# Expert retrieval in two layers: gathered rows against whole tables streamed through TensorE

## What is computed

```python
q = (xb @ w_q).reshape(n, 8, 2, 128)                       # 8 heads, two halves
s = einsum('thpk,pnk->thpn', q, sub_keys)                  # 128 scores for each half
s_top, i_top = top_k(s, 16)
cand_s = s_top[:, :, 0, :, None] + s_top[:, :, 1, None, :]
cand_i = i_top[:, :, 0, :, None] * 128 + i_top[:, :, 1, None, :]
best_s, best_pos = top_k(cand_s.reshape(n, 8, -1), 16)     # 16 of 256 pairs
idx = take_along_axis(cand_i.reshape(n, 8, -1), best_pos)
gate = softmax(best_s)
act = gelu(einsum('thkd,td->thk', down[idx], xb))
out = einsum('thk,thkd->td', gate * act, up[idx])
```

## Time and profile before

| what | us |
|---|---|
| three runs | 2356.95, 2358.21, 2359.39 |
| profiled execution, span | 2356.5 |
| of this, PE busy | 2048.2 |
| DVE busy | 1155.2 |
| ACT busy | 647.4 |
| POOL busy | 601.8 |

### The profile page before, as it was taken

The page is one execution under the profiler, slowest core; times in us unless marked ns, Lnnn a source line. Parts: engine busy times, 40 slices in busy tenths (PEclk is TensorE's granted clock), DMA queues, the critical chain, the costliest instruction groups (busy, mean ns, idle before and its releaser), DMA issues.

```text
span 2356.5 us, 21481 instructions
## 1 busy us (share of the span) xinstructions
PE 2048.2 (87%) x7609; PEld 981.8 (42%) x7609; DVE 1155.2 (49%) x2857; ACT 647.4 (27%) x1813; POOL 601.8 (26%) x516
## 2 busy tenths in 40 slices
PE   7999998777777888998777777779999999999998
PEld 3455664232323336664223223334445544444443
DVE  2335766676667556766676667544534311111111
ACT  2242333332333222333332333332432210000001
POOL 0001344444444431344444444430000000000000
PEclk9999999999999998999999999999999999999999
DMA  9696999999999987999999999996313399999996
GB/s 391 252 423 246 407 417 420 420 416 422 406 420 413 409 347 293 406 420 421 421 420 417 412 421 412 407 396 262 119 57 135 160 402 427 428 426 428 427 427 262
DMA packets 98201, 860.93 MB, mean 365 GB/s; under 512 B 11406, under 2 KB 11534, under 8 KB 12844
## 3 DMA queue, kind: packets, MB, share of 16 engines
q0 software_dynamic: 73728, 536.90, 55.3%
q1 hardware_dynamic: 24364, 322.62, 32.9%
HBM read 858.44 MB, written 1.05 MB: 365 GB/s over the span
## 4 chain that ended last, share of the span: by engine, by line
PE 55%; DMA 29%; DVE 7%; ACT 4%; issue 3%; POOL 2%; POOLq 0%; SPq 0%; DVEq 0%; ACTq 0%
DMA arena<-in_experts,arena 16%; PE bank L2348 16%; PE bank L2012 15%; DMA ring<-in_experts,arena 9%; PE bank L2699 9%; PE bank L2745 4%; PE bank L2709 2%; PE bank L2116 2%; DVE arena L1479 2%; DMA arena<-in_w_up 2%; ACT arena L903 2%; POOL arena L696 1%; PE bank L2128 1%; POOL ring L696 1%; DVE ring L1479 1%
## 5 line engine op out<-in xcount | busy, mean ns | idle before, releaser
L2348 PE MATMUL bank<-arena 128*128 128x512 f32 x1040 | 486.3, 612 | 128.6 <-ACT arena L903 128.6
L2348 PE MATMUL bank<-ring,arena 128*128 128x512 f32 x1008 | 472.1, 612 | 116.5 <-ACT arena L903 116.4
L696 POOL DMA_INDIRECT arena<-in_experts,arena x260 | 299.8, 1153 | 638.2 <-PE bank L2348 331.7
L1479 DVE SCALAR_TENSOR_TENSOR arena<-arena,h 128x1024 f32<-128x1024 f32 x260 | 318.7, 1226 | 231.1 <-DMA arena<-in_experts,arena 230.1
L1479 DVE SCALAR_TENSOR_TENSOR ring<-ring,h 128x1024 f32<-128x1024 f32 x252 | 308.9, 1226 | 217.0 <-DMA ring<-in_experts,arena 216.4
L696 POOL DMA_INDIRECT ring<-in_experts,arena x252 | 301.8, 1198 | 329.5 <-PE bank L2348 288.4
L2348 PEld LDWEIGHTS bank<-arena 128*128 128x128 f32 x1040 | 191.2, 193 | 401.6 <-ACT arena L903 201.4
L2348 PEld LDWEIGHTS bank<-ring,arena 128*128 128x128 f32 x1008 | 185.5, 193 | 384.2 <-ACT arena L903 193.9
L894 ACT ACTIVATE arena<-arena 128x2 f32<-128x2 f32 x256 | 52.1, 203 | 838.5 <-DVE arena L1479 456.1
L2699 PE MATMUL bank<-ring,arena 128*64 128x512 f32 x768 | 223.4, 592 | 2.0 <-ACT arena L1096 1.2
L903 ACT ACTIVATE arena<-const,arena 128x128 f32<-128x128 f32 x512 | 177.6, 394 | 8.4
(11 more groups left out here) (430 smaller groups left out, 1811.8 us busy)
## 6 DMA issues: line engine op xcount, KB each, us to landing
ring<-in_w_gate SPq DMA_DIRECT2D x32, 2048.0 KB, 14.8
ring<-in_mod_w SPq DMA_DIRECT2D x20, 2048.0 KB, 11.8
arena<-in_w_up SPq DMA_DIRECT2D x16, 2048.0 KB, 20.9
arena<-in_w_down SPq DMA_DIRECT2D x16, 2048.0 KB, 15.8
ring<-in_w_up SPq DMA_DIRECT2D x16, 2048.0 KB, 16.4
ring<-in_w_down SPq DMA_DIRECT2D x16, 2048.0 KB, 11.5
ring<-in_w_in SPq DMA_DIRECT2D x9, 2048.0 KB, 7.3
ring<-in_peer_w_q SPq DMA_DIRECT2D x8, 2048.0 KB, 12.3
```

The lines of the kernel that those rows point to most:

```text
L696: pool.indirect_dma_start(out=gslot(l, n), out_offset=None, in_=a["experts"], in_offset=bass.IndirectOffsetOnAxis(ap=idx_all[:, t, at:at + ...
L1479: ins = v.scalar_tensor_tensor(out=row, in0=row, scalar=1.0, in1=h[:, t], op0=ALU.mult, op1=ALU.mult, accum_out=act[:, t, HEAD * hh + k:HE ...
L2348: ins = pe.matmul(bank[2 * t + c][:, :], diag[:, PER * (j % 2) + k], row[:, 512 * c:512 * c + 512], start=j % (GROUPS // NT) == 0 and k == ...
```

## The change

Both tables of a layer are read whole, once, in pieces of 1 MB, and nothing is gathered.

- The 16384 experts are 128 columns j of 128 experts i. A piece of `down` holds two columns. PE multiplies it by `hT` (8 matmuls of 256 tokens each), and ACT puts gelu of it into `kept`, 256 numbers a partition for each j, experts on the partitions. 112 columns fit (`KEPT`); the last 16 wrap onto the first once these are summed.
- A piece of `up` holds two columns as well; PE multiplies the kept products with it into the four output banks (`sums`, 4 matmuls of 512 columns for each j).
- In between, the kept products are multiplied by the gates. The picks (i, j, gate) are transposed, so that a column is a token and its 128 picks are the partitions. For 8 tokens at a time DVE makes the one-hots of i (128 wide) and of j (64 wide, half of the keys), POOL multiplies the one-hot of j by the gate, PE multiplies the two (8 matmuls, one a token, 64 columns each), which gives each token's gates by expert in a bank, and DVE multiplies 64 kept columns by it. There are 2 halves x 32 such groups a layer, with two buffers of each kind.
- Pieces go through three places (`streams`), and the last five of a layer through five more. SP's list has the pieces in the order of use, and between them the late rows of `mod_w` (all four in layer 0 now), the constants, `pool_w` and the first three chunks of `w_in`.
- Top-k works on two heads of one tile at a time, always, eight blocks a layer in a row, with 14 steps.
- The out projection is complete, and both tiles are normalised and transposed, before the first query. At a layer's end the last 8 pieces of `up` are summed for tile 0 first, then for tile 1. `keep_warm` is gone.

```diff
+TILE = 256
+KEPT = 112
+PAIR_TILES = KEYS // 2
+KEPT_PAIRS = KEPT // 2
+WRAPPED = PAIR_TILES - KEPT_PAIRS
+TAIL = 8
+STREAMS = 3
+PIECE = 2048
...
+QUERY_AT = {0: 0, 4: 1, 10: 2, 17: 3}
+ROW_AT_PAIR = {6: 16, 9: 17, 12: 18, 15: 19}
+def piece_order():
+    order = []
+    for p in range(KEPT_PAIRS):
+        if p in QUERY_AT:
+            order += [("q", 2 * QUERY_AT[p]), ("q", 2 * QUERY_AT[p] + 1)]
+        order.append(("d", p))
+    for p in range(WRAPPED):
+        order += [("u", p), ("d", KEPT_PAIRS + p)]
+    order += [("u", p) for p in range(WRAPPED, PAIR_TILES)]
+    return order
...
+    return (n + 1) % STREAMS if n < PIECES - HELD else n - (PIECES - HELD) + STREAMS
...
+EXP_AT = {29: 0, 32: 1}
+TURN_PICKS_AT = {31: 0, 34: 1}
+SPREAD = KEPT_PAIRS - 33
+GROUPS_AT = {33 + p: tuple(range(GROUPS * p // SPREAD, GROUPS * (p + 1) // SPREAD)) for p in range(SPREAD)}
+GROUPS_BEHIND = {p: tuple(range(4 * (p - WRAPPED) // 3, 4 * (p - WRAPPED + 1) // 3)) for p in range(WRAPPED, PAIR_TILES // 2)}
+TOTAL_AT = [{33 + n: n for n in range(10)}, {33: 10, 34: 11}]
...
+            def load_piece(l, n):
+                kind, i = ORDER[n]
+                k = place_of(n)
+                if k < STREAMS:
+                    same = [m for m in range(PIECES) if place_of(m) == k]
+                    at = same.index(n)
+                    if at or l:
+                        sp.wait_ge(S["piece_done"], PIECES * (l if at else l - 1) + same[at - 1] + 1)
+                    elif k == 0:
+                        sp.wait_ge(S["mixed"], NT)
+                else:
+                    sp.wait_ge(S["piece_done"], done(l, "u", KEPT_PAIRS // 2 + 7 + 4 * (k - STREAMS)))
+                sp.dma_start(streams[k], piece_source(l, kind, i)).then_inc(p_landed[k], 16)
...
+            for n in range(PIECES):
+                load_piece(0, n)
+                kind, i = ORDER[n]
+                if kind == "d" and i in (2, 5, 8, 11):
+                    load_lone(i // 3)
+                if (kind, i) == ("u", 36):
+                    sp.wait_ge(S["w_made"], 2 * GROUPS)
+                    sp.dma_start(own, a["const"][:, band_at:band_at + 2048]).then_inc(S["in_const"], 16)
+                if (kind, i) == ("u", 40):
+                    load_weights("pool", 1)
+            for n in range(PIECES):
+                load_piece(1, n)
+                if ORDER[n] == ("u", 36):
+                    load_weight(wat["in2"])
+                if ORDER[n] == ("u", 41):
+                    load_weight(wat["in2"] + 1)
+                if ORDER[n] == ("u", 46):
+                    load_weight(wat["in2_third"])
...
+                for half in range(2):
+                    for g in range(GROUPS):
+                        n = group_no(l, half, g)
+                        pool.wait_ge(S["hot_j_made"], n + 1)
+                        hot = hot_j[:, n % 2]
+                        weight = picksT[:, 2, GROUP * g:GROUP * g + GROUP].unsqueeze(2).to_broadcast([P, GROUP, HALF_KEYS])
+                        pool.tensor_tensor(hot, hot, weight, ALU.mult).then_inc(S["hot_made"], 1)
...
+                def one_hots(half, g):
+                    n = group_no(l, half, g)
+                    at = slice(GROUP * g, GROUP * g + GROUP)
+                    keys = cst("iota")[:, HALF_KEYS * half:HALF_KEYS * half + HALF_KEYS]
+                    if half == 0 and g in (0, GROUPS // NT):
+                        v.wait_ge(S["picks_ev"], NT * l + g // (GROUPS // NT) + 1)
+                    if n >= 2:
+                        v.wait_ge(S["g_done"], n - 1)
+                    i_hot, j_hot = hot_i[:, n % 2], hot_j[:, n % 2]
+                    v.tensor_tensor(i_hot, bc(cst("iota"), 1, GROUP), bc(picksT[:, 0, at], 2, KEYS), ALU.is_equal)
+                    v.tensor_tensor(j_hot, bc(keys, 1, GROUP), bc(picksT[:, 1, at], 2, HALF_KEYS), ALU.is_equal).then_inc(S["hot_j_made"], 1)
+                def weigh(half, g):
+                    n = group_no(l, half, g)
+                    if g == 0:
+                        v.wait_ge(S["s_ev"], PAIR_TILES * l + PAIR_TILES // 2 * (half + 1))
+                    v.wait_ge(S["g_done"], n + 1)
+                    runs = [(0, 0, HALF_KEYS)] if half == 0 else [(0, HALF_KEYS, KEPT - HALF_KEYS), (KEPT - HALF_KEYS, 0, KEYS - KEPT)]
+                    gates_of_keys = bank[6 + n % 2][:, :].rearrange("p (u j) -> p j u", u=GROUP)
+                    for at, v0, width in runs:
+                        part = kept_run(v0, width)[:, :, GROUP * g:GROUP * g + GROUP]
+                        ins = v.tensor_tensor(part, part, gates_of_keys[:, at:at + width], ALU.mult)
+                    ins.then_inc(S["w_made"], 1)
+                for n in range(HEADS):
+                    for step in range(STEPS):
+                        top_k(n, step)
+                    if l == 0 and n == 4:
+                        v.wait_ge(S["modp"], 4 + 20)
+                        v.tensor_tensor(mrows2, mrows1, bank[3][:, :], ALU.add).then_inc(S["rows_made"], 1)
+                gates(0)
+                for half in range(2):
+                    for g in range(GROUPS):
+                        one_hots(half, g)
+                        if (half, g) == (0, 1):
+                            gates(1)
+                        if g:
+                            weigh(half, g - 1)
+                    weigh(half, GROUPS - 1)
...
+                def add_experts(t):
+                    if t == 0:
+                        v.wait_ge(S["first_summed"], l + 1)
+                    else:
+                        v.wait_ge(S["piece_done"], PIECES * (l + 1))
+                    for c in range(2):
+                        link(v.tensor_tensor(h[:, t, 512 * c:512 * c + 512], bank[2 * t + c][:, :],
+                                             mod[:, 5, 512 * c:512 * c + 512], ALU.mult))
+                    v.tensor_tensor(x[:, t], x[:, t], h[:, t], ALU.add).then_inc(S["x_peer"], 1)
+                for t in range(NT):
+                    add_experts(t)
+                    tile_mean(("n1_1", "nf1")[l], t)
+                    if l == 0:
+                        tile_norm("n1_1", t, x, h, mod[:, 1], mod[:, 0])
+                    else:
+                        tile_gained("nf1", t, x, gvec[:, 1])
+                        tile_mean("nmix", t)
+                        tile_gained("nmix", t, h, gvec[:, 0])
...
-                    pool.indirect_dma_start(
-                        out=gslot(l, n), out_offset=None, in_=a["experts"],
-                        in_offset=bass.IndirectOffsetOnAxis(ap=idx_all[:, t, at:at + 1], axis=0)).then_inc(
-                        S[f"gathered{place_of(n)}"], 16)
...
+                def score_out(n):
+                    act_.wait_ge(S["ps"], HEADS * l + n + 1)
+                    if n >= 4:
+                        act_.wait_ge(S["block_done"], HEADS * l + n - 3)
+                    act_.activation(flat(s16[:, n % 4]), bank[6 + n % 2][:, :], ACT.Copy).then_inc(S["ps_ev"], 1)
+                def products_out(p):
+                    act_.wait_ge(S["piece_done"], done(l, "d", p))
+                    act_.activation(kept_pair(p), bank[4 + p % 2][:, :], ACT.Gelu_apprx_tanh).then_inc(S["s_ev"], 1)
...
-            project_out1(0, 0)
-            project_out1(0, 1)
-            project_out1(1, 0)
+            for t in range(NT):
+                for c in range(2):
+                    project_out1(t, c)
+            row_parts(15)
...
+                    tile_transposes(h, t)
+                for p in range(KEPT_PAIRS):
+                    if p in QUERY_AT:
+                        c = QUERY_AT[p]
+                        query(2 * c)
+                        query(2 * c + 1)
+                    products(p)
+                    if p in QUERY_AT:
+                        scores(2 * c)
+                        scores(2 * c + 1)
+                    if l == 0 and p in ROW_AT_PAIR:
+                        late_row(ROW_AT_PAIR[p] - LATE_ROWS[0])
+                    if p in TURN_PICKS_AT:
+                        turn_picks(TURN_PICKS_AT[p])
+                    for g in GROUPS_AT.get(p, ()):
+                        spread_gates(0, g)
...
+                def products(p):
+                    wait_piece(pe, l, "d", p)
+                    if p >= 2:
+                        pe.wait_ge(S["s_ev"], PAIR_TILES * l + p - 1)
+                    w = piece(l, "d", p).rearrange("p (j k n) -> p j k n", j=2, k=KT)
+                    for j in range(2):
+                        ins = accumulate(bank[4 + p % 2][:, TILE * j:TILE * j + TILE], [(w[:, j, q], hT[:, q, :]) for q in range(KT)])
+                    ins.then_inc(S["piece_done"], 1)
...
+                def spread_gates(half, g):
+                    n = group_no(l, half, g)
+                    pe.wait_ge(S["hot_made"], n + 1)
+                    if half == 0 and g < 2:
+                        pe.wait_ge(S["ps_ev"], HEADS * l + HEADS)
+                    else:
```

(71 more changed lines are left out.)

687 lines of the change are left out of this document (217 added, 470 removed).

## The result

| | before | changed |
|---|---|---|
| median, 4 runs each, us | 2358.68 (2356.95 to 2359.39) | 3165.23 (3162.21 to 3167.97) |
| profiled execution, span | 2356.5 | 3164.6 |
| PE busy | 87% | 98% |
| DMA share in the retrieval stages | 0.99, 1.01 | 0.39, 0.40 |

The ratio is 1.342 [1.340, 1.344]. The forecast was 2140 with 2100 to 2225 and 0.96 for faster: wrong in sign and far outside the range.

A forecast was written before the change was run, and what follows sets the result against it. The prediction took transfers to bound the kernel before and PE after: layers of 542.8 and 534.9 us plus 25 us of stalls each put the z projection 217.9 us earlier, giving 2140 us, range 2100 to 2225.

The forecast's parts named there:

- What bounds the kernel before: transfers: Retrieval stages before: DMA share 0.99 and 1.01, PE's 3.7 us lying within a 5.0 us period of two gathers.
- The price of PE's work: PE in both layers: 0.43 us per matmul of 512 columns, 0.2156 of 256; layers of 542.8 and 534.9 us.
- The sum exceeds the transfer, so the bound moves to PE: Retrieval layers: PE's 542.8 and 534.9 us exceed 340 us of transfer, so PE binds if nothing starves it.
- The stream: Table pieces: landing in 4.9 us, hidden; loads put between them hold it up 6 us in layer 0, 4 in layer 1.
- 10 us of waiting at the two ends: Each layer's end: the last six pieces start only after piece 55, so PE waits 5 us a layer.
- The gate chain: DVE, GpSimd and PE per 8 tokens: DVE 2.6 us, GpSimd 1.2, period up to 3.4, about PE's own pace.
- 20 us booked for handovers within the chain: Gate groups: 0.15 us for each of 64 groups, 10 us a layer, where two groups stand behind one pair.
- 8 at the ends of the halves: End of each half of a layer: sums wait for the last weighing, 2 x 2 us a layer.
- The lock that the forecast weighed: Gate one-hots: DVE with two SBUF inputs and GpSimd exclude each other, period 3.3 to 3.4 us; without it some 15 us lower.
- The 2 us of waiting for picks: Layer 1: top-k picks ready at 144.5 us, PE reaching their turning at 142; no wait in layer 0.
- The edges: Outside the layers: first query 206.2 plus 2, handover 31.3, z projection 2.3 us after layer 1, the rest unchanged.
- The rivals: Stalls: gate chain binds (0.20), 2223 or 2285 us; stream starves PE (0.15), 2200 to 2496; no stall (0.03), 2092.

The follow-up runs named there:

- e2: Changed kernel without right-half sums for 126 of 128 keys and with products from 4 of 8 blocks of h; output wrong: 2308.66 us, 0.979 of before.
- e5: Changed kernel with products, sums and spreads in bf16, ACT casting the pieces, both tiles summed together to a layer's end: 2009.27 us, 0.851 of before.
- e3: Changed kernel, float32, with the gates' multiply moved from GpSimd to DVE: 3168.82 us, 3.6 us above the changed kernel.
- e6: The bf16 version of the changed kernel (e5) with the gates' multiply moved from GpSimd to DVE: 2036.94 us, 0.863 of before.

## Why the prediction was wrong, step by step

1. *What bounds the kernel before: transfers.* Not tested by itself. The period of 5.0 us against PE's 3.7 stands in the earlier trace rows. The DMA share did fall, to 0.39 rather than 0.65, at 141 GB/s: about the forecast's bytes over nearly twice its time.
2. *The price of PE's work: the step that failed.* In the forecast's words, "16 matmuls of 512 columns take 7.13 us": they are 8 matmuls in 16 records. Products, sums, queries, scores, spreads, late rows, totals and gains were all booked at half: 540.8 and 532.9 us were missing in the two layers. Measured is 0.86 us for a matmul of 512 columns, not 0.43. I called it the firmest number, and it had no error bar at all.
3. *It could be read before.* A group of the kernel before has, in the code, two picks times two halves, four matmuls; the earlier trace rows has x8 for it, and the forecast said "eight matmuls". The description of the kernel before has the same slip twice: line 2348 issues four matmuls a group, not eight, and `keep_warm(8, 0)` eight, not 16. The whole layer was a second check: the sums of the change are 512 matmuls of 128x512 a layer, exactly as many, of the same shape, as line 2348 issued before (128 groups of four). Those took 128 x 3.7 = 474 us of a layer, and the forecast gave the same work 219.9.
4. *The sum exceeds the transfer, so the bound moves to PE.* Right, by far more than thought.
5. *The stream.* Landing 4.9 forecast, 4.8 measured, with PE taking about twice as long over a piece as the forecast had it. In e2, where PE spends half of that on each piece again, it waits 12.7 us in all for pieces. In the changed kernel late rows and copies of `w_in` held nothing back, and of 10 us of waiting at the two ends none showed, but the slow PE hid all that.
6. *The gate chain.* GpSimd's multiply at 1.07 us against 1.2 taken; DVE's parts 1.32, 0.71 and about 0.7. Of the 20 us booked for handovers within the chain none occurred, and of the 8 at the ends of the halves 3.6. At PE's real pace that proves little; e2 and e5 show the chain at a period of 2.8 us when nothing else holds it, so at the forecast's 3.4 to 3.5 it would probably have been hidden too. The lock that the forecast weighed shows as 0.38 us a group, not as a period of 3.3 to 3.4: DVE's multiply from PSUM runs beside the first 0.4 us of GpSimd's, and only the next one-hots are held. The 2 us of waiting for picks did not show either (and 132 and 11.6 add up to 143.6, not 144.5).
7. *The edges.* First query 208.0 against 208.2, handover 29.8 against 31.3, z start 1.6 against 2.3, the rest 768.8 against 769.1. These were differences of times taken from the same trace, with no count in them.
8. *The rivals* were about stalls. None asked whether the unit price was right, though a change that moves the bound onto one engine stands or falls with it.

## What to carry to other kernels

Before a row's duration is divided by its count, compare the count with the loops of the code for one line that both show: here a float32 matmul is two records, a bf16 matmul and a transpose are one. When a change swaps bytes for TensorE work, price that work by a stretch of the old kernel with the same number of matmuls of the same shape, not by a unit price alone; halving the bytes of a transfer-bound stage in float32 cost some 1075 us of matmuls a layer, and the same design in bf16 was 15% faster than before. Moving an operation to an idle engine is worth nothing while another engine is 98% busy (e3), and gains little where its work stretches that of the engine relieved (e6: 0.31 us of 0.69).

## What the runs showed of the hardware that I had not expected

- A float32 matmul costs four times a bf16 one at 256 and 512 columns (0.43 against 0.107 us, 0.86 against 0.213) and seven times at 64 columns behind a new 128x128 weight (0.216 against 0.03).
- A DVE instruction with two SBUF inputs stretches beside GpSimd, but only by part of the overlap: 1219 ns alone, 1322 on average in the changed kernel, where 30 of 128 are stretched, 1600 in e5, where 114 are. In the lines of e5 shown under e6 the overlap is 0.60 us and the stretch 0.46. One with an input from PSUM does not stretch (0.67). The Trainium skill's SBUF — State Buffer page (Who interferes with whom) has both sides of this rule, and the traces agree.
- A GpSimd multiply of 128x512 elements takes 1.07 us in float32 and in bf16 alike.
